# Token-major sums of squares, small roots and spreading products in all norms of a two-layer DiT block

## The reference, cut to what matters

```python
def rmsnorm(x, w):
    y = xf * lax.rsqrt(jnp.mean(xf * xf, axis=-1, keepdims=True) + EPS)
    return (y * w)

hl = rmsnorm(x, norm_mix_w[layer]) * (1.0 + sc1) + sh1
x = x + g1 * mixer(hl, hc)
x = x + g2 * swiglu(rmsnorm(x, norm_ffn_w[layer]) * (1.0 + sc2) + sh2)
...
return rmsnorm(x, final_norm_w)
```

## Time and profile before

| what | value |
|---|---|
| median of three runs | 4062.64 us |
| profiled execution | 4066.5 us |
| its span in the trace | 4064.7 us |
| TensorE matmuls busy | 3520.0 us (87%) |
| VectorE busy | 1589.4 us (39%) |
| ScalarE busy | 1073.4 us (26%) |
| GpSimd busy | 646.9 us (16%) |
| mean granted TensorE clock | 0.924 |

### The profile page before, as it was taken

The page is one execution under the profiler, slowest core; times in us unless marked ns, Lnnn a source line. Parts: engine busy times, 40 slices in busy tenths (PEclk is TensorE's granted clock), DMA queues, the critical chain, the costliest instruction groups (busy, mean ns, idle before and its releaser), DMA issues. The chain is left out here.

```text
span 4064.7 us, 54588 instructions
## 1 busy us (share of the span) xinstructions
PE 3520.0 (87%) x20668; PEld 2942.1 (72%) x20668; DVE 1589.4 (39%) x2595; ACT 1073.4 (26%) x1927; POOL 646.9 (16%) x758
## 2 busy tenths in 40 slices
PE   5989666968697999999998989667866879999998
PEld 3778565846585888888885878556755758888886
DVE  3466634632324222222236465634621342222324
ACT  2343123621204121211213343123511131221112
POOL 1134633221100000000001234532222000000000
PEclk8999887988698999999999999888987889999999
DMA  4455374069201111111111465373096111111111
GB/s 161 138 182 187 91 206 130 27 181 303 99 21 37 36 41 36 36 41 36 40 37 71 151 197 164 107 205 110 18 274 198 42 36 47 49 49 46 46 52 57
DMA packets 281909, 405.19 MB, mean 100 GB/s; under 512 B 108675, under 2 KB 184707, under 8 KB 280966
## 3 DMA queue, kind: packets, MB, share of 16 engines
q1 hardware_dynamic: 277894, 392.39, 31.1%
q0 software_dynamic: 3840, 10.49, 0.7%
HBM read 292.08 MB, written 110.70 MB: 99 GB/s over the span
## 5 line engine op out<-in xcount | busy, mean ns | idle before, releaser
L901 PE MATMUL ffn_bank<-ffn_h_hi,ffn_w_hi 128*128 128x512 f32 (+1 forms) x1760 | 650.7, 370 | 18.1 <-DVE ffn_h_lo L314 18.1
L904 PE MATMUL ffn_bank<-ffn_h_lo,ffn_w_hi 128*128 128x512 f32 (+1 forms) x1760 | 650.0, 369 | 0.0
L905 PE MATMUL ffn_bank<-ffn_h_hi,ffn_w_lo 128*128 128x512 f32 (+1 forms) x1760 | 649.4, 369 | 0.0
L811 PE MATMUL frt_acc<-frt_w_hi,frt_h_hi 128*128 128x472 f32 x960 | 374.8, 390 | 48.5 <-DVE frt_w_lo L688 27.5
L901 PEld LDWEIGHTS ffn_bank<-ffn_h_hi,ffn_w_hi 128*128 128x128 f32 x1760 | 333.3, 189 | 75.8 <-DVE ffn_h_lo L314 18.1
L904 PEld LDWEIGHTS ffn_bank<-ffn_h_lo,ffn_w_hi 128*128 128x128 f32 x1760 | 333.2, 189 | 55.4
L905 PEld LDWEIGHTS ffn_bank<-ffn_h_hi,ffn_w_lo 128*128 128x128 f32 x1760 | 333.0, 189 | 55.7
L811 PE MATMUL frt_acc<-frt_w_hi,frt_h_lo 128*128 128x472 f32 x960 | 368.1, 383 | 0.0
L811 PE MATMUL frt_acc<-frt_w_lo,frt_h_hi 128*128 128x472 f32 x960 | 365.3, 381 | 0.0
L895 DVE TENSOR_TENSOR ffn_w_lo<-ffn_raw,ffn_w_hi 128x1024 fp32r<-128x1024 f32 x132 | 161.8, 1226 | 502.0 <-ACT ffn_w_hi L891 496.8
L901 PE MATMUL ffn_bank<-ffn_a_hi,ffn_w_hi 128*128 128x512 f32 (+1 forms) x880 | 324.3, 369 | 0.8 <-DVE ffn_a_lo L969 0.8
(11 more groups left out here) (310 smaller groups left out, 5699.5 us busy)
## 6 DMA issues: line engine op xcount, KB each, us to landing
ffn_raw<-w_ffn SPq DMA_DIRECT2D x132, 512.0 KB, 3.2
x<-ada_w SPq DMA_DIRECT2D x20, 2048.0 KB, 10.9
proj<-frt_out SPq DMA_DIRECT2D x120, 236.0 KB, 2.0
x<-proj SPq DMA_DIRECT2D x60, 384.0 KB, 4.5
frt_raw<-w_in SPq DMA_DIRECT2D x96, 236.0 KB, 4.5
pack<-frt_side SPq DMA_DIRECT2D x80, 256.0 KB, 2.5
scn_fd<-feat SPq DMA_DIRECT2D x40, 384.0 KB, 8.2
met_pr<-proj SPq DMA_DIRECT2D x20, 704.0 KB, 5.5
```

Source lines behind the costliest of these rows:

```text
L811: mm = pe.matmul(acc[q % NA][:, 0:GW], a[:, k, tok], b[:, k, :], start=(k == 0 and i == 0), stop=(k == KC - 1 and i == 2))
L901: mm = pe.matmul(out, w_hi, b_hi, start=first, stop=False)
L904: pe.matmul(out, w_hi, b_lo, start=False, stop=False)
L905: return pe.matmul(out, w_lo, b_hi, start=False, stop=last)
```

## The change

The squares become the weights of the product and two columns of ones move, tile by tile of 128 tokens, so the sums come out with the tokens on the partitions, two equal columns for each tile. Root and reciprocal are taken of 2 x 4 columns (2 x 2 in the slice of 256), and a product with broadcast weights and an identity spreads the reciprocals over the partitions into the bank that held the sums; VectorE's scaling reads them there. ScalarE squares two chunks of the next slice beside each of the first four roundings, and takes the next slice's root before the sixth; VectorE inverts it there. The next slice's first scaling now stands ahead of a slice's last remainder. In the feed-forward stage GpSimd squares the last slice into two buffers of its own. The final norm has the same sums, roots and spreading, with its squares on ScalarE as before. The core of the diff (the call sites that only hand over the identity are left out):

```diff
@@ -242,17 +242,17 @@
                 m.gpsimd_end(pool)
 
 
-def normed(nc, st, x, scale, mod, shift0, lo, hi_t, lo_t, ones, eps, bufs=None, ms=None):
+def normed(nc, st, x, scale, mod, shift0, lo, hi_t, lo_t, ones, ident, eps, bufs=None, ms=None, far=None):
 
 
     slices = token_slices(lo)
-    if bufs is None:
-        bufs = ([st.sb(f"sq{u}", [P, 512])[:] for u in range(2)], [st.sb(f"scaled{u}", [P, 512])[:] for u in range(2)],
-                [st.sb(f"inv{s}", [P, n])[:] for s, (t0, n) in enumerate(slices)])
-        ms = [st.ps(f"ms{s}", [P, 512]) for s in range(len(slices))]
-    sq, scaled, inv = bufs
-    squared, summed, rooted, inverted = st.sem("squared"), st.sem("summed"), st.sem("rooted"), st.sem("inverted")
+    NS = len(slices)
+    sq, scaled = bufs
+    root, rstd = [[st.sb(f"{n}{s}", [P, 4, 2]) for s in range(NS)] for n in ("root", "rstd")]
+    squared, summed, rooted, inverted, spread = st.sem("squared"), st.sem("summed"), st.sem("rooted"), st.sem("inverted"), st.sem("spread")
+    squared_far = st.sem("squared_far")
     scaled_s, rounded, h_ready = st.sem("scaled"), st.sem("rounded"), st.sem("h_ready")
+    near = NS - 1 if far else NS
 
     def act_norm(act, between=None):
         def square(s, k):
...
@@ -262,9 +262,10 @@
                 act.wait_ge(summed, i - 1)
             act.activation(sq[i % 2][:, 0:n], x[:, k, t0:t0 + n], ACT.Square).then_inc(squared, 1)
 
-        def root(s):
+        def take_root(s):
+            tiles = slices[s][1] // P
             act.wait_ge(summed, (s + 1) * KC)
-            act.activation(inv[s], ms[s][:, 0:slices[s][1]], ACT.Sqrt, bias=eps[:]).then_inc(rooted, 1)
+            act.activation(root[s][:, 0:tiles, :].rearrange("p t n -> p (t n)"), ms[s][:, 0:2 * tiles], ACT.Sqrt, bias=eps[:]).then_inc(rooted, 1)
 
         def round_(s, k):
             t0, n = slices[s]
...
@@ -275,35 +276,60 @@
 
         for k in range(KC):
             square(0, k)
-        root(0)
+        take_root(0)
         if between:
             between(act)
-        for s in range(len(slices)):
+        for s in range(NS):
             for k in range(KC):
-                if s + 1 < len(slices):
-                    square(s + 1, k)
+                if s + 1 < near and k < KC // 2:
+                    square(s + 1, 2 * k)
+                    square(s + 1, 2 * k + 1)
+                if s + 1 < NS and k == KC // 2 + 1:
+                    take_root(s + 1)
                 round_(s, k)
-            if s + 1 < len(slices):
-                root(s + 1)
+
+    def pool_norm(pool):
+        t0, n = slices[NS - 1]
+        for k in range(KC):
+            if k >= 2:
+                pool.wait_ge(summed, (NS - 1) * KC + k - 1)
+            pool.tensor_tensor(far[k % 2][:, 0:n], x[:, k, t0:t0 + n], x[:, k, t0:t0 + n], ALU.mult).then_inc(squared_far, 1)
 
     def pe_sum(pe, s):
         t0, n = slices[s]
         for k in range(KC):
-            pe.wait_ge(squared, s * KC + k + 1)
-            pe.matmul(ms[s][:, 0:n], ones[:], sq[(s * KC + k) % 2][:, 0:n], start=(k == 0), stop=(k == KC - 1)).then_inc(summed, 1)
+            if s < near:
+                pe.wait_ge(squared, s * KC + k + 1)
+                src = sq[(s * KC + k) % 2]
+            else:
+                pe.wait_ge(squared_far, k + 1)
+                src = far[k % 2]
+            for t in range(n // P):
+                mm = pe.matmul(ms[s][:, 2 * t:2 * t + 2], src[:, t * P:(t + 1) * P], ones[:, 0:2], start=(k == 0 and t == 0), stop=(k == KC - 1 and t == n // P - 1))
+            mm.then_inc(summed, 1)
+
+    def pe_spread(pe, s):
+        t0, n = slices[s]
+        pe.wait_ge(inverted, s + 1)
+        for t in range(n // P):
+            mm = pe.matmul(ms[s][:, t * P:(t + 1) * P], rstd[s][:, t, 0:1].broadcast_to([P, P]), ident, start=True, stop=True)
+        mm.then_inc(spread, 1)
 
     def dve_norm(dve):
+        def invert(s):
+            tiles = slices[s][1] // P
+            dve.wait_ge(rooted, s + 1)
+            dve.reciprocal(rstd[s][:, 0:tiles, :], root[s][:, 0:tiles, :]).then_inc(inverted, 1)
+
         def scale_one(i):
             s, k = i // KC, i % KC
             t0, n = slices[s]
             v = 1 if t0 < CTX else 0
             if k == 0:
-                dve.wait_ge(rooted, s + 1)
-                dve.reciprocal(inv[s], inv[s]).then_inc(inverted, 1)
-                dve.wait_ge(inverted, s + 1)
+                dve.wait_ge(spread, s + 1)
             if i >= 2:
                 dve.wait_ge(h_ready, i - 1)
-            dve.scalar_tensor_tensor(scaled[i % 2][:, 0:n], x[:, k, t0:t0 + n], scale[:, k, v:v + 1], inv[s],
+            dve.scalar_tensor_tensor(scaled[i % 2][:, 0:n], x[:, k, t0:t0 + n], scale[:, k, v:v + 1], ms[s][:, 0:n],
                                      ALU.mult, ALU.mult).then_inc(scaled_s, 1)
 
         def rest(i):
...
@@ -314,18 +340,17 @@
             dve.scalar_tensor_tensor(lo_t[:, k, t0:t0 + n], scaled[i % 2][:, 0:n], mod[:, shift0 + k, v:v + 1],
                                      hi_t[:, k, t0:t0 + n].bitcast(F32), ALU.add, ALU.subtract).then_inc(h_ready, 1)
 
-        parts = len(slices) * KC
+        parts = NS * KC
+        invert(0)
         scale_one(0)
         for i in range(parts):
-            if (i + 1) % KC == 0:
-                rest(i)
-                if i + 1 < parts:
-                    scale_one(i + 1)
-            else:
+            if i + 1 < parts:
                 scale_one(i + 1)
-                rest(i)
-
-    return act_norm, pe_sum, dve_norm, h_ready
+            if i % KC == KC // 2 + 1 and i // KC + 1 < NS:
+                invert(i // KC + 1)
+            rest(i)
+
+    return act_norm, pool_norm, pe_sum, pe_spread, dve_norm, h_ready
 
 
 def front(nc, layer, x, x_copy, w_in, proj, mod, amix, ones, eps, conv_w, small, mats, tri, pack, feat, diag, inv, tot):
...
@@ -854,11 +878,13 @@
                                         mm = pe.matmul(bank[i, at:at + 64], khT[d, pair, i], rhs[d, pair, i], start=True, stop=True)
                             mm.then_inc(s[name], 1)
 
-                pe_sum(pe, 0)
-                pe_sum(pe, 1)
+                for part_ in range(2):
+                    pe_sum(pe, part_)
+                    pe_spread(pe, part_)
                 for q in range(SLOTS):
                     if q == 2:
                         pe_sum(pe, 2)
+                        pe_spread(pe, 2)
                     project(q)
                     for phase, j in phases(q):
                         part(phase, j)
...
@@ -923,9 +949,9 @@
         prod = st.sb("prod", [P, TOK])
         bank = [[st.ps(f"bank{i}{s}", [P, 512]) for s in range(len(slices))] for i in range(2)]
 
-        bufs = ([st.sb(f"sq{u}", [P, 512])[:] for u in range(2)], [prod[:, 0:512], prod[:, 512:1024]],
-                [sil[:, t0:t0 + ln] for t0, ln in slices])
-        act_norm, pe_sum, dve_norm, h_ready = normed(nc, st, x, affn, mod, 3 * KC, lo, h_hi, h_lo, ones, eps, bufs, bank[1])
+        bufs = ([st.sb(f"sq{u}", [P, 512])[:] for u in range(2)], [prod[:, 0:512], prod[:, 512:1024]])
+        act_norm, pool_norm, pe_sum, pe_spread, dve_norm, h_ready = normed(nc, st, x, affn, mod, 3 * KC, lo, h_hi, h_lo, ones, ident, eps, bufs, bank[1],
+                                                                           [sil[:, 0:512], sil[:, 512:1024]])
         w = WeightUnits(st, units)
 
         full = [[st.sem(f"full{i}{s}") for s in range(len(slices))] for i in range(2)]
...
@@ -1023,6 +1049,10 @@
             def _(sp):
                 w.load_all(sp, LAST + REST + 1)
 
+            @block.gpsimd
+            def _(pool):
+                pool_norm(pool)
+
             @block.scalar
             def _(act):
                 act_norm(act, between=lambda act: w.round(act, 0, 0))
...
@@ -2197,15 +2228,15 @@
                         add(n, u)
 
 
-def final(nc, x, norm_w, out, ones, eps):
+def final(nc, x, norm_w, out, ones, ident, eps):
 
     with Stage(nc, "fin") as st:
         nw = st.sb("nw", [P, KC])
         sq = [st.sb(f"sq{i}", [P, 512]) for i in range(2)]
-        root, inv = st.sb("root", [P, 512]), [st.sb(f"inv{i}", [P, 512]) for i in range(2)]
+        root, rstd = [[st.sb(f"{n}{i}", [P, 4, 2]) for i in range(2)] for n in ("root", "rstd")]
         y = st.sb("y", [P, KC, LAT])
         ms = [st.ps(f"ms{s}", [P, 512]) for s in range(2)]
-        s = signals(st, "set_in squared summed rooted inverted done stored")
+        s = signals(st, "set_in squared summed rooted inverted spread done stored")
         with nc.Block() as block:
             @block.sync
             def _(sp):
...
@@ -2226,15 +2257,21 @@
                             act.wait_ge(s["summed"], i - 1)
                         act.activation(sq[i % 2][:], x[:, k, t:t + 512], ACT.Square).then_inc(s["squared"], 1)
                     act.wait_ge(s["summed"], (sl + 1) * KC)
-                    if sl:
-                        act.wait_ge(s["inverted"], 1)
```

(14 more changed lines are left out.)

14 lines of the change are left out of this document (7 added, 7 removed).

## The result

The changed kernel takes 4108.45 us (median of four runs, 4105.61 to 4110.28); the kernel before, on the same chip, 4064.51 us. The ratio is 1.0107, 95% interval 1.009 to 1.0125: 44 us slower, where 31 were forecast, and just above the range.

A forecast was written before the change was run, and what follows sets the result against it. TensorE, busy 87% of the span, was taken as the bound outside the norms. Norm terms 3.7+3.5+6.5+6.5+10.2 = 30.4, say +31, on the median 4062.64 gave 4093.6 us; own range 4080 to 4107, reached down to 4064 for 8 in 10.

The forecast's parts named there:

- Sums: All norms: eight loads a chunk take 1.78 us at 1.2 GHz, as in the earlier trace's gated stage; not the scan stage's 0.97.
- The front's third sum: Second layer's front stage: sum after two projections, first part still at 2.4 GHz, between 7.8 and 14.2 us, taken as 10.
- The rival that the sums keep 2.4 GHz: All norms: the clock stays up over the sums, giving 4057 us, between 4050 and 4062; chance 0.15.
- Roots, reciprocals, spreading: All norms: root 0.25 us, reciprocal 0.20, spreading 1.0 to 2.0; a slice's factor ready 2.7 us after its sum at 1.2 GHz.
- Scaling from PSUM at nothing: VectorE's scaling in the norms: reading PSUM instead of SBUF costs nothing, between 0 and 0.1 us each.
- GpSimd at nothing: Last feed-forward slice: GpSimd's squares, some 1.35 us each, meet VectorE, but cost it nothing where TensorE paces the slice.
- First feed-forward stage, +3.7: First feed-forward norm: ends 4.7 us later, 1.0 comes back from a higher clock afterwards; net +3.7 us.
- Second, +3.5: Second feed-forward norm: ends at 3318.8 against TensorE's restart at 3314.94, part comes back from the clock; net +3.5 us.
- five short stretches: The norms heading two front and two feed-forward stages, and the final norm: the only places the change can move time.
- Front stages, +6.5 each: Both front stages: ScalarE's first copy, which TensorE waits for, comes 8 us later, less 1.5 for a higher clock.
- Final norm, +10.2: Final norm: its sums, factors and eight outputs end at 4071.9 against 4061.67, +10.2 us.
- the rival of a partly raised clock: All norms: the clock is up in part of the sums, giving 4078 us, between 4068 and 4086; chance 0.12.

The follow-up runs named there:

- e4_filler: The changed kernel with one more, unused fp32 product of 256 columns ahead of each chunk's sums in the feed-forward and final norms; 4151.2 us.
- e1: The changed kernel with the feed-forward stages' small root and reciprocal tiles laid behind the weight buffers, no instruction changed; 4088.1 us.
- e5: e1 with the last feed-forward slice squared by ScalarE like the others, GpSimd idle; 4091.3 us.
- e7: e1 with both front stages given the norm of the kernel before (512-column sums, old order); 4076.4 us.
- e8: e1 with only the front stages' order put back to that of the kernel before, their sums still token-major; 4085.5 us.
- p256: The kernel before with 256 unused bytes a partition ahead of the feed-forward stages' weight buffers; 4067.5 us, run once.
- e12: The kernel before with 64 unused bytes a partition ahead of the feed-forward stages' first tile, shifting weights and streamed tiles together; 4068.8 us, run once.
- e2_pad: The kernel before with an unused tile ahead of the feed-forward weight buffers, 192 bytes a partition in the first layer, 128 in the second; 4079.7 us.
- e6_order: The kernel before with only the new order of the norms; sums, roots and reciprocals 512 columns wide as before; 4079.3 us.
- e3_final_old: The changed kernel with the final norm of the kernel before; 4098.7 us.
- e10_filler512: e1 with one more, unused fp32 product of 512 columns ahead of each chunk's sums in the feed-forward and final norms; 4141.2 us.

## Why the prediction missed

What the prediction says of the norms was right: the granted clock is at 0.50 over nearly all of the sums, a chunk takes 1.71 us (1.78 assumed, from the earlier trace rows), and the norms end later in spite of small roots and reciprocals. What it missed lies outside the norms. Point by point:

- *Sums.* Right. The choice between the earlier trace rows was the one that mattered, and e4_filler has both in one place: 1.71 and 0.95 a chunk. The front's third sum, part of it at 2.4 GHz, took 9.36 us where 10 was said. The rival that the sums keep 2.4 GHz fell: TensorE was busy for 2.00 of 2.00 us at 0.50. The Trainium skill ("TensorE: Matmul & The Clock Gate", Part 1) says that activity releases the throttle; by that rule the rival would have won, and the measurement goes against it for these sums.
- *Roots, reciprocals, spreading.* 0.27, 0.20 and 2.07 us, against 0.25, 0.20 and up to 2.0. From a sum's end to the first scaling it is 4095.19 - (4078.83+13.65) = 2.71 us; 2.7 was said.
- *Scaling from PSUM at nothing.* Right in the final norm (eight outputs in 5.36 us, 5.39 before), wrong in the front stages, where GpSimd works beside it: 0.48 us in place of up to 1.40. The prediction left this gain out; slice 0 waits for TensorE there, so it hardly shows in the changed kernel.
- *GpSimd at nothing.* Right, and its squares take 1.04 us, less than the 1.35 estimated. The lock that the Trainium skill's page "SBUF — State Buffer", section "SBUF: two separate sides", tells of agrees with 1.00 to 1.28 us for a remainder beside a square and 0.75 alone.
- *First feed-forward stage, +3.7.* With the weights in place (e1, e5, e7, e8) it is 961.3 on average against 958.3 (before, p256, e12): +3.0.
- *Second, +3.5.* By the same kernels 763.9 against 761.2: +2.7. In the changed kernel it was +21.3. **This is the step that failed.** The prediction opens with "what this change can move lies in five short stretches", the norms. It costed each instruction that the change adds and none of its allocations; "Second feed-forward norm" was costed, and the main products behind it were taken as they were. The two kinds of small tile moved the weights by 128 bytes against the streamed tiles: 16.1 us in e2_pad, 19.8 here (783.1 against 763.3).
- *Front stages, +6.5 each.* The six profiles with the changed front stage average 448.3 and 447.3, the nine with the old one 442.8 and 440.6: +5.5 and +6.7. The size was right, the working only half: I had charged the late end of slice 0 to the sums alone, and e6_order shows that the order would cost as much without them.
- *Final norm, +10.2.* +8.3 between the two profiles, 10 by e3_final_old.
- *What lies between.* Not in the sum: the stages between were 8.8 us shorter in the changed kernel's profile and 5.4 in e1_layout's. That part of the front stages' loss is given back there is not shown: e7_front_old, with the front stages of before, has the same 1368.2 us as the changed kernel, and profiles scatter by 12.

The norms' terms add up to 30.4 as forecast and 26.2 as measured (5.5 + 6.7 + 3.0 + 2.7 + 8.3); by the medians e1_layout, which has the norms' cost alone, is 23.6 above the kernel before. The other 20.4 us (4108.5 - 4088.1) are the weights' place. The range had no case for it.

Two slips in the prediction's sums do not bear on this. The norms have 13 slices, not 12. And half of 6.4 us in nine sums is 29 us, not 15, so the rival of a partly raised clock would have stood at about 4065 and not at 4078.

## What to carry to other kernels

A product with the data as weights and two columns moving costs a full weight load (eight in 1.71 us), and a run of them here left TensorE at 1.2 GHz, or brought it there within a few microseconds, however busy it was; price such a form at the low clock, and cut its loads (one pass in place of two) if the sums can spare the low part. A change that allocates a tile moves every tile behind it: allocate new small tiles behind the weights and the tiles that stream against them, and compare the product count of equal windows in the untouched main loop before blaming the edited code. An order that reads as free can put a long operation ahead of the one that the next engine waits for.

## What the runs showed of the hardware that was not expected

- The pace of dense fp32r products at full clock hung on the byte distance between the weight tiles and the stage's tiles ahead of them: 178 products in 40 us at distances shifted by 0 or 256 bytes, 173 or 174 at 64 and 128; in the first feed-forward stage 192 bytes cost 3.1 us and 64 bytes 15.4.
- TensorE's clock fell from 2.4 to 1.2 GHz while it was busy without a gap with two-column products: within the first 4 us in the final norm, and after projections in the front stage between 96 and 100 us, 4 to 8 us after these products began. 256-column fp32 products among them did not hold it (e4_filler).
- VectorE's scaling beside GpSimd took up to 1.40 us for 256 columns with its factor in SBUF, and 0.48 with it in PSUM.
- Runs of one kernel (e10_filler512) spread over 52 us, where the others stay within 20.
